# One fused encoder step on Trainium2: attention re-cut into steps of one chunk and one key group, with four query tiles placed between them

## The chip, the core and the metric

The kernel runs on one core of one Trainium2 chip. The metric is the device time of one execution in microseconds (us). The engines are named as in the profile: PE (matrix products), PEld (its weight loads), DVE (vector), ACT (scalar), POOL (GpSimd) and SP (issues most DMAs). All operands are float32. In projections each operand is split into a rounded part (`hi`, type fp32r) and a rest (`lo`), and three products `hi*hi + hi*lo + lo*hi` are summed; inside attention plain float32 products are used.

## What is computed

The reference is a two-layer trunk for two request groups: one prompt of 512 rows and 8 streams of 16 new rows, so 640 rows of width 1024. Layer 0 is gated linear attention and a convolutional FFN; layer 1 is windowed attention over shared keys and values, and again the FFN. The change touches the windowed attention and the end of both mixers' output projections. Cut to that part:

```
def sink_attention(q, k, v, valid, sinks):
    s = einsum('bqngd,bknd->bngqk', q, k)
    m = maximum(max(s, -1), sink)
    e = exp(s - m)
    p = e / (sum(e, -1) + exp(sink - m))
    return einsum('bngqk,bknd->bqngd', p, v)
# prompt: 8 chunks of 64 queries; a chunk sees its own 64 keys and the 128 before it (fewer for chunks 0 and 1)
# streams: 16 queries see 128 cached keys and their own 16
# 16 query heads of 64 in 2 key groups (8 heads share one key and value head)
x = x + attention(rmsnorm(x) @ w_q, ...) @ w_o
x = x + conv_ffn(rmsnorm(x))
```

## The kernel before

The program is written out by hand as one instruction list per engine, with semaphores between them. Each engine works its own list in order, so the order in the source is the schedule. The residual `X` and its two parts `XH`, `XL` lie with features on partitions: 8 tiles of 128 x 640. A projection to 128 output features is a **tile**: `fm_tile` (L359 to L373, products at L368) runs 8 feature blocks x 3 products x 2 halves of 320 columns, 48 matmuls into one of four pairs of PSUM banks; `fm_half` (L375, L379) does one half of it. Weight tiles are brought by SP in pairs (`later_piece`, L864), rounded by ACT (`round_tile`, L344, L348), and their rest is taken by DVE (`rest_tile`, L351, L355); four weight slots rotate.

**Attention stage** (`att_*`, L870 to L1261). PE makes keys and values (`tm_unit`), four query tiles, transposes keys and cached keys (L944, L952), then makes the other four query tiles (L955, products at L368). DVE scales each query tile into `QF` (L1135) and copies the transposed keys into `KTD` (L1125) and `KCT` (L1126, L1131). Then come 40 **steps**: 32 of the prompt (chunk `c`, two neighbouring query tiles, which is four heads of one key group) and 8 of one stream each. For a step:

- PE `scores` (L959): two products, one per half of the array's rows (64 each), into two banks (L972); in a stream step two products of full height with zero-padded queries `QZ` (L979).
- DVE `maxima` (L1142): a row maximum over both banks (L1147), the sink (L1149, L1151) and the sign (L1152).
- ACT `exponentials` (L1216): two exponentials with a running sum (L1223) and one for the sinks (L1224).
- DVE `normalise` (L1154): sum (L1157), reciprocal (L1159), two scalings of the probabilities (L1163).
- PE `transposes` (L984, L992), ACT `to_sbuf` (L1226, L1237 or L1241), PE `values` (L996): per half of the probabilities one product over 128 window keys and one over 64 own keys (L1007); in a stream step one over 128 cached keys (L1016) and one over 16 new ones (L1018). The value operand `VZ` carries 64 zero columns, so that each product fills all 128 output partitions.
- ACT `round_out` (L1244, L1248) and DVE `rest_out` (L1166, L1170) write the result as `XH`, `XL`.

The loops are skewed: in round `n`, PE does `scores(n)`, `transposes(n-2)`, `values(n-3)`; DVE `maxima(n)`, `normalise(n-1)`, `rest_out(n-4)`; ACT `round_out(n-4)`, `to_sbuf(n-2)`, `exponentials(n)`. Scores, transposed probabilities and results each alternate between two places, so `scores(n)` waits for `exponentials(n-2)`. DVE also copies the stream queries into `QZ` (L1176), and POOL has cleared `QZ` and the zero columns (L907).

After the last steps PE makes the output projection: the first half of its tile 0 between the last steps (L1030), the other half (L1036), and tiles 1 to 7 (L1038). DVE adds each tile to `X` (`add_x`, L493). **Resplit**: when all eight tiles are done, ACT rounds the eight blocks of the new `X` (`round_x`, L436) and DVE takes the rests (`rest_x`, L440), because `XH` is still read by the last tile; the FFN's first tile waits for each block's rest. The same two helpers (`add_and_resplit`, L453, and `square_and_resplit`, L463) serve the output projection of layer 0.

```
            act.wait_ge(full, u0 + KT)
            for k in range(KT):
                if k == 2:
                    round_tile(act, n0 + 4 + KT - 1)
                ...
                round_x(act, k, vec)
```

Of the kernel before, what the change touches and what calls it, by code (L numbers as in the profile page):

```python
# [45 lines left out]
def build(nc, A, O):  # L46
    ctx = ExitStack()
    with ctx:
# [63 lines left out]
        NM = sb("neg_max", [128, 2, 2])  # L112
        SE = sb("sink_exp", [128, 2, 2])
        ES = sb("exp_sum", [128, 2, 2])
# [63 lines left out]
        P = at("probs", [128, 2, 512], F32, e_area)  # L178
        PT = at("probs_cols", [128, 2, 512], F32, e_area + 4096)
        KTD = at("keys_cols", [128, KVH, SEQ], F32, e_area + 8192)  # L180
        VZ = at("v_0_v", [128, TT - 1, KVH, 3 * HD], F32, e_area + 12288)
        QZ = at("q_0_q", [128, NS, KVH, 2, 4, SL], F32, e_area + 18432)
# [3 lines left out]
        V4 = at("v_new_rows", [128, KVH, 2, HD], F32, d_area + 5120)  # L186
        VN = at("v_new", [SL, NS, KVH, 2, HD], F32, d_area + 6144)
        VCD = at("cache_v", [128, NS, KVH, 2, HD], F32, DRAW_AREA)
        VS = at("v_0_v_shifted", [128, TT - 1, KVH, 3 * HD], F32, k_area)
# [16 lines left out]
        free = sem("free")  # L206
        hi_done = sem("hi_done")
# [79 lines left out]
        a_pt = sem("a_pt")  # L287
        a_o = sem("a_o")
# [23 lines left out]
        U_AO = U_KC + 6  # L312
# [18 lines left out]
        NATT = (TT - 1) * KT + NS  # L331
# [27 lines left out]
        def fm_tile(pe, n0, u0, i=0, wstep=4, ustep=4, fresh=None, beside=None):  # L359
            pe.wait_ge(lo_done, n0 + 1 + wstep * i)  # L360
            if u0 >= 4:
                pe.wait_ge(free, u0 - 3 + ustep * i)
            for k in range(KT):
                if fresh is not None:
                    pe.wait_ge(xl_done, fresh + k + 1)
                for a, (w, x) in enumerate(((WH, XH), (WH, XL), (WL, XH))):
                    for f in range(2):
                        mm = pe.matmul(PS[:, 2 * (u0 % 4) + f, 0:HALF], w[:, n0 % 4, k, :],  # L368
                                       x[:, k, f * HALF:(f + 1) * HALF],
                                       start=(k == 0 and a == 0), stop=(k == KT - 1 and a == 2))  # L370
            if beside is not None:
                mm = beside()
            mm.then_inc(full, 1)  # L373
# [79 lines left out]
        def add_and_resplit(v, n0, u0, vec, base):  # L453
            for j in range(KT):
                add_x(v, j, u0 + j)
                if j < KT - 1:
                    rest_tile(v, n0 + 4 + j)
            for k in range(KT):
                if k == 2:
                    rest_tile(v, n0 + 4 + KT - 1)  # L460
                rest_x(v, k, vec, base)

        def square_and_resplit(act, n0, u0, norm, vec):  # L463
# [5 lines left out]
            act.wait_ge(full, u0 + KT)  # L469
            for k in range(KT):  # L470
                if k == 2:
                    round_tile(act, n0 + 4 + KT - 1)
                if k == 4:
                    act.wait_ge(free, u0 + KT)
                    square_x(act, KT - 1, norm)
                if k == KT - 1:
                    act.wait_ge(free, u0 + KT)
                round_x(act, k, vec)

# [390 lines left out]
        def att_sp(sp):  # L870
# [12 lines left out]
            sp.dma_start(VS[0:CH, :], VZ[CH:128, :]).then_inc(s_vs, 16)  # L883
            sp.dma_start(VS[CH:128, 0:TT - 2], VZ[0:CH, 1:TT - 1]).then_inc(s_vs, 16)
            for dup in range(2):
                for g in range(KVH):
                    sp.dma_start(VCD[:, :, g, dup, :], A["cache_v"][:, :, g, :].rearrange("s k d -> k s d")).then_inc(s_vn, 16)
# [6 lines left out]
            for s in range(NS):  # L894
                r = slice(SL * s, SL * s + SL)
                sp.dma_start(O["k_s"][s, WIN - SL:WIN], KD[r, TT - 1, :, 0, :]).then_inc(s_out, 16)
                sp.dma_start(O["v_s"][s, WIN - SL:WIN], V4[r, :, 0, :]).then_inc(s_out, 16)
            sp.dma_start(O["k_p"][0], KD[:, TT - 2, :, 0, :]).then_inc(s_out, 16)
            sp.dma_start(O["v_p"][0], VZ[:, TT - 2, :, 0:HD]).then_inc(s_out, 16)
# [7 lines left out]
        def att_pool(pool):  # L907

            pool.wait_ge(free, U_KV)
            pool.wait_ge(s_tout, 128)  # L910
            pool.memset(QZ[:, :, :, :, :, :], 0.0).then_inc(azero, 1)
            pool.memset(VZ[:, :, :, HD:2 * HD], 0.0).then_inc(azero, 1)

# [5 lines left out]
        def att_pe(pe):  # L919
# [17 lines left out]
            for j in range(1, 4):  # L937
                fm_tile(pe, T_AQ + j, u_q(j))
# [16 lines left out]
            for j in range(4, 8):  # L955
                fm_tile(pe, T_AQ + j, u_q(j))
            pe.wait_ge(s_vs, 16 * 2)

            def scores(n):  # L959
                if n >= 2:  # L960
                    pe.wait_ge(a_ex, n - 1)
                if n < 2:

                    pe.wait_ge(free, u_q(5 + n) + 1)
                if n == 3:
                    pe.wait_ge(free, u_q(7) + 1)
                if n < NATT - NS:
                    c, m, g = step_of(n)
                    k0, nk = window(c)
                    for a in range(2):  # L970
                        h = slice(HD * a, HD * a + HD)
                        mm = pe.matmul(PS[:, score_bank(n) + a, 0:nk], QF[h, m // 2, c, :, :].rearrange("p m q -> p (m q)"),  # L972
                                       KTD[h, g, k0:k0 + nk], start=True, stop=True, tile_position=(HD * a, 0))
                else:
                    s = n - (NATT - NS)
                    if s == 0:
                        pe.wait_ge(qz, 16)
                    for g in range(KVH):
                        mm = pe.matmul(PS[:, score_bank(n) + g, 0:WIN + SL],  # L979
                                       QZ[:, s, g, :, :, :].rearrange("p e m t -> p (e m t)"), KCT[:, g, s, :],  # L980
                                       start=True, stop=True)
                mm.then_inc(a_sc, 1)

            def transposes(n):  # L984
# [3 lines left out]
                if n >= 2:  # L988
                    pe.wait_ge(a_pt, n - 1)
                for a in range(2):  # L990
                    for x, k in enumerate(key_parts(n)):
                        mm = pe.transpose(PS[0:k, prob_bank(n), 256 * a + 128 * x:256 * a + 128 * x + 128],  # L992
                                          P[:, n % 2, 256 * a + 128 * x:256 * a + 128 * x + k], ident[:, :])
                mm.then_inc(a_tr, 1)

            def values(n):  # L996
                pe.wait_ge(a_pt, n + 1)
                if n >= 2:
                    pe.wait_ge(a_ol, n - 1)
                b = out_bank(n)  # L1000
                if n < NATT - NS:
                    c, m, g = step_of(n)
                    ops = [(a, x, k) for a in range(2) for x, k in enumerate(key_parts(n))]
                    for j, (a, x, k) in enumerate(ops):
                        vv = VS if c % 2 and c > 1 else VZ
                        t = max(c // 2 - 1, 0) + x
                        mm = pe.matmul(PS[:, b, 0:128], vv[0:k, t, g, HD * a:HD * a + 128],  # L1007
                                       PT[0:k, n % 2, 256 * a + 128 * x:256 * a + 128 * x + 128],
                                       start=(j == 0), stop=(j == len(ops) - 1))
                else:  # L1010
                    s = n - (NATT - NS)
                    if s == 0:
                        pe.wait_ge(s_vn, 16 * (NS + 4))
                    for g in range(KVH):
                        o = PS[:, b, 128 * g:128 * g + 128]
                        pe.matmul(o, VCD[:, s, g, :, :].rearrange("p e d -> p (e d)"),  # L1016
                                  PT[:, n % 2, 256 * g:256 * g + 128], start=True, stop=False)
                        mm = pe.matmul(o, VN[:, s, g, :, :].rearrange("p e d -> p (e d)"),  # L1018
                                       PT[0:SL, n % 2, 256 * g + 128:256 * g + 256], start=False, stop=True)
                mm.then_inc(a_o, 1)  # L1020

            for n in range(NATT + 3):
                if n < NATT:
                    scores(n)
                if n == NATT + 1:
# [3 lines left out]
                    pe.wait_ge(a_ol, 4 * HALF // CH)  # L1029
# [3 lines left out]
                if n >= 3:  # L1033
                    values(n - 3)
            pe.wait_ge(a_ol, NATT)
            fm_half(pe, T_AO, U_AO, 1).then_inc(full, 1)  # L1036
            for j in range(1, KT):
                fm_tile(pe, T_AO + j, U_AO + j)  # L1038

        def score_bank(n):
            return 2 * ((U_AO + n % 2) % 4)

        def prob_bank(n):
            return 2 * ((U_AO + 2) % 4) + n % 2
# [3 lines left out]

        def u_q(j):  # L1050
            return U_Q + j + (4 if j >= 4 else 0)

        def step_of(n):
            c, m = n // 4, 2 * (n % 4)
            return c, m, m // 4
# [4 lines left out]
        def key_parts(n):  # L1063

            if n >= NATT - NS:
                return [WIN, SL]
            nk = window(step_of(n)[0])[1]
            return [nk] if nk <= 128 else [128, nk - 128]

        def heads_out(n, a):  # L1070

            b = out_bank(n)
            if n < NATT - NS:
                c, m, _ = step_of(n)
                return [PS[:, b, 0:128].rearrange("p (m q) -> p m q", m=2)] + \
# [1096 lines left out]
```

## Time and profile before

| | us |
|---|---|
| median of 3 runs (lowest, highest) | 1546.15 (1545.23, 1547.86) |
| the profiled execution: its time | 1542.32 |
| its span, first to last instruction | 1540.6 |
| last four query tiles begin | 862.76 |
| 40 attention steps | 891.1 to about 997 |
| output tiles 1 to 7 begin | 1002.87 |
| FFN of layer 1, first tile begins | 1054.08 |

### The profile page before, as it was taken

How to read it: one execution, taken by the hardware profiler on the slowest of the kernel's cores; microseconds unless marked ns; L12 is line 12 of the kernel's file. 1: busy time of each engine (PE TensorE's matmuls, PEld its weight loads, DVE VectorE, ACT ScalarE, POOL GpSimd, SP SyncE). 2: the span in 40 equal slices, each digit the busy share in tenths (PEclk: the TensorE clock that was granted, in tenths of full speed). 3: DMA queues.
4: the chain of work that ended last, by engine and by line, in shares of the span. 5: the costliest groups of instructions: out<-in, count | busy, mean ns of one | idle time of the engine just before them, and what ended most of it. 6: DMA issues, size and time to landing. Idle time of an engine off the chain costs nothing.

```text
span 1540.6 us, 26157 instructions
## 1 busy us (share of the span) xinstructions
PE 1487.6 (97%) x10213; PEld 1442.7 (94%) x10213; DVE 975.0 (63%) x1748; ACT 563.4 (37%) x989; POOL 169.4 (11%) x186
## 2 busy tenths in 40 slices
PE   7999998999999999999998989999999999999996
PEld 6988998999999999999998967899999999999996
DVE  4366676448666666676577378536766666666655
ACT  4145354434232323233343157524333332323222
POOL 1013220121000000000032000021000000000000
PEclk9999999999999999999999989999999999999999
DMA  6421333432222122112206300021222222212102
GB/s 227 128 83 57 112 102 101 136 110 83 82 82 82 54 82 82 58 51 81 83 1 142 116 28 1 13 83 55 84 81 82 82 82 82 82 64 72 54 1 93
DMA packets 104360, 122.17 MB, mean 79 GB/s; under 512 B 13315, under 2 KB 96201, under 8 KB 104025
## 3 DMA queue, kind: packets, MB, share of 16 engines
q1 hardware_dynamic: 104188, 121.27, 24.4%
q8 instruction: 43, 0.70, 0.2%
q14 instruction: 21, 0.16, 0.0%
q10 hardware_dynamic: 108, 0.03, 0.0%
HBM read 109.43 MB, written 11.95 MB: 79 GB/s over the span
## 4 chain that ended last, share of the span: by engine, by line
PE 91%; DVE 5%; ACT 2%; issue 1%; POOL 0%; DMA 0%; SPq 0%; DVEq 0%; ACTq 0%
PE ps L368 54%; PE ps L529 18%; PE ps L1764 7%; PE ps L1007 2%; DVE x_lo L440 1%; PE ps L547 1%; PE ps L992 1%; PE ps L379 1%; PE ps L393 1%; PE ps L1809 1%; PE ps L972 1%; PE ps L1822 1%; PE ps L1846 1%; PE ps L1842 0%; DVE x_res L493 0%
## 5 line engine op out<-in xcount | busy, mean ns | idle before, releaser
L368 PE MATMUL ps<-x_hi,w_hi 128*128 128x320 f32 x1888 | 431.3, 310 | 7.4 <-DVE x_lo L440 6.9
L368 PE MATMUL ps<-x_lo,w_hi 128*128 128x320 f32 x1888 | 430.2, 309 | 0.0
L368 PE MATMUL ps<-x_hi,w_lo 128*128 128x320 f32 x1888 | 430.2, 309 | 0.0
L368 PEld LDWEIGHTS ps<-x_hi,w_hi 128*128 128x128 f32 x1888 | 315.4, 188 | 9.4 <-issue 4.7
L368 PEld LDWEIGHTS ps<-x_hi,w_lo 128*128 128x128 f32 x1888 | 315.7, 188 | 0.0
L368 PEld LDWEIGHTS ps<-x_lo,w_hi 128*128 128x128 f32 x1888 | 315.6, 188 | 0.0
L348 ACT ACTIVATE w_hi<-w_raw 128x1024 fp32r<-128x1024 f32 x138 | 145.0, 1060 | 423.4 <-PE ps L368 382.2
L493 DVE TENSOR_TENSOR x_res<-x_res,ps 128x640 f32<-128x640 f32 x192 | 153.7, 817 | 130.1 <-PE ps L368 66.1
L355 DVE TENSOR_TENSOR w_lo<-w_raw,w_hi 128x1024 fp32r<-128x1024 f32 x138 | 169.7, 1236 | 33.6 <-ACT w_hi L348 26.4
L611 DVE TENSOR_TENSOR up_rows<-ps,rstd_cols 128x320 f32<-128x320 f32 x88 | 43.1, 490 | 164.6 <-PE ps L368 164.6
L529 PE MATMUL ps<-gated_hi,d_hi 128*128 128x320 f32 x640 | 145.8, 309 | 0.0
L529 PE MATMUL ps<-gated_lo,d_hi 128*128 128x320 f32 x640 | 145.7, 309 | 0.0
L529 PE MATMUL ps<-gated_hi,d_lo 128*128 128x320 f32 x640 | 145.6, 309 | 0.0
L807 POOL TENSOR_TENSOR tail_cols<-up_rows,ones 128x4 f32 (+1 forms) x44 | 51.2, 1164 | 827.7 <-DVE up_rows L613 773.5
L529 PEld LDWEIGHTS ps<-gated_hi,d_hi 128*128 128x128 f32 x640 | 107.0, 188 | 0.0
L529 PEld LDWEIGHTS ps<-gated_lo,d_hi 128*128 128x128 f32 x640 | 106.9, 188 | 0.0
L529 PEld LDWEIGHTS ps<-gated_hi,d_lo 128*128 128x128 f32 x640 | 106.9, 188 | 0.0
L745 ACT ACTIVATE d_hi<-d_raw 128x512 fp32r<-128x512 f32 x88 | 54.7, 628 | 138.7 <-PE ps L529 138.7
L1764 PE MATMUL ps<-w_hi,x_hi 128*128 128x256 f32 x320 | 93.5, 292 | 4.8 <-DVE log_gate L1595 2.6
L733 ACT ACTIVATE conv_out<-up_rows,conv_taps 128x656 f32<-128x656 f32 x88 | 82.2, 935 | 37.6 <-DVE up_rows L613 35.8
L1764 PE MATMUL ps<-w_lo,x_hi 128*128 128x256 f32 x320 | 91.7, 286 | 0.0
L1764 PE MATMUL ps<-w_hi,x_lo 128*128 128x256 f32 x320 | 91.6, 286 | 0.0
(269 smaller groups left out, 1901.3 us busy)
## 6 DMA issues: line engine op xcount, KB each, us to landing
w_raw<-in_ffn_w_up_dram SPq DMA_DIRECT2D x44, 1024.0 KB, 5.2
d_raw<-in_ffn_w_down_dram SPq DMA_DIRECT2D x22, 1024.0 KB, 5.0
w_raw<-in_gla_w_in_dram SPq DMA_DIRECT2D x12, 1024.0 KB, 6.1
seq_states<-in_state_gla_dram SPq DMA_DIRECT2D x4, 1024.0 KB, 5.5
out_dram<-seq_states SPq DMA_DIRECT2D x4, 1024.0 KB, 8.3
w_raw<-in_gla_w_out_dram SPq DMA_DIRECT2D x4, 1024.0 KB, 5.3
w_raw<-in_att_w_q_dram SPq DMA_DIRECT2D x4, 1024.0 KB, 6.8
w_raw<-in_att_w_o_dram SPq DMA_DIRECT2D x4, 1024.0 KB, 5.0
```

What stands on the lines that cost most here:

```text
L348: act.activation(WH[:, n0 % 4, :, :], WRAW[:, p0 % 2, :, half:half + 128], ACT.Copy).then_inc(hi_done, inc)
L355: v.tensor_tensor(WL[:, n0 % 4, :, :], WRAW[:, p0 % 2, :, half:half + 128], f32(WH[:, n0 % 4, :, :]), ALU.subtract).then_inc(lo_done, inc)
L368: mm = pe.matmul(PS[:, 2 * (u0 % 4) + f, 0:HALF], w[:, n0 % 4, k, :], x[:, k, f * HALF:(f + 1) * HALF], start=(k == 0 and a == 0), stop=(k ...
L379: mm = pe.matmul(PS[:, 2 * (u0 % 4) + f, 0:HALF], w[:, n0 % 4, k, :], x[:, k, f * HALF:(f + 1) * HALF], start=(k == 0 and a == 0), stop=(k ...
L493: v.tensor_tensor(halves(X[:, m, :]), halves(X[:, m, :]), unit(u0), ALU.add).then_inc(free, inc)
L529: mm = pe.matmul(PS[:, 2 * (w % 4) + f, 0:HALF], wt[:, k, 128 * m:128 * m + 128], y[:, k, f * HALF:(f + 1) * HALF], start=(k == 0 and a == ...
L611: v.tensor_tensor(UB[:, j, 2:2 + HALF], PS[:, b, 0:HALF], RB[:, 0:HALF], ALU.mult)
L733: act.activation(CB[:, j, :], UB[:, j, 0:CC], ACT.Identity, scale=CWT[:, 0, bass.ds(c, 1)], bias=CWT[:, 3, bass.ds(c, 1)]).then_inc(t0_don ...
L745: act.activation(DH[:, :, 256 * c:256 * c + 256], DRAW[:, :, 256 * c:256 * c + 256], ACT.Copy).then_inc(dhi, 1)
L807: pool.tensor_tensor(to[:, :, 0:2], UB[:, a, SEQ:SEQ + 2], ones[:, 0:4].rearrange("p (a r) -> p a r", a=2), ALU.mult)
L1007: mm = pe.matmul(PS[:, b, 0:128], vv[0:k, t, g, HD * a:HD * a + 128], PT[0:k, n % 2, 256 * a + 128 * x:256 * a + 128 * x + 128], start=(j ...
L1764: mm = pe.matmul(PS[:, VR_B[m % 2], 0:DV], x[:, k, 128 * t:128 * t + 128], w[:, n0 % 4:n0 % 4 + 2, k, :], start=(k == 0 and a == 0), stop= ...
```

## The change

- A prompt step is one chunk and one whole key group: eight heads, four products of scores, 16 steps ordered group by group (`ATT_STEPS`). A stream step takes two streams: 4 steps. 20 steps in place of 40; four row sums and maxima per step in place of two.
- Query tiles 4 to 7 (the second group's) are no longer made before the steps. Each of the first eight steps is followed on PE by one half tile (`query_half`), evicted by `query_out`; these use the second pair of score banks, so up to step 8 there is one pair for scores, and `scores(n)` waits for `exponentials(n-1)`.
- `scores(0)` waits until all transposed keys, the cached ones too, are copied (`U_KC + 2`).
- Values: without zero columns. Products have 64 output columns of the array each and 256 moving columns: two over 128 window keys, two over 64 own keys (each in its own quarter of the array). `VP`, `VS` hold values once; a third copy fills the shifted rows.
- Stream queries lie packed in `QS`, written by POOL (a product with ones); scores and values of streams use 64-column pieces. `QZ` and its clearing are gone. Cached values come in one DMA in place of four.
- Transposed probabilities have one place for the window part (copied by ACT) and one for the own part (copied by DVE, `own_to_sbuf`).
- One broadcast product normalises all four heads' blocks.
- Results of the first eight steps go to `QF` (where the first group's queries were) and are split later, tile by tile, in rounds 12 to 15 (`rest_first` and ACT's rounding), since `XH` is still read by the query halves.
- The four output weight tiles formerly prepared under the query tiles are prepared in rounds 2, 4, 6 and 8.
- Output tile 1's first half is made before the second half of tile 0.
- Resplit, in both layers: the last output tile releases each block of `XH` as it is read (`x_free`), and seven of eight blocks are split under that tile.

```diff
-        NATT = (TT - 1) * KT + NS
+        ATT_STEPS = [(c, g) for g in range(KVH) for c in range(SEQ // CH)]
+        NCH, NPR = SEQ // CH, len(ATT_STEPS)
+        NATT = NPR + NS // 2
...
         def fm_tile(...):
-            if beside is not None:
-                mm = beside()
+                if release and k < KT - 1:
+                    mm.then_inc(x_free, 1)
...
         def add_and_resplit(v, n0, u0, vec, base):
-            for j in range(KT):
+            for j in range(KT - 1):
                 add_x(v, j, u0 + j)
-                if j < KT - 1:
-                    rest_tile(v, n0 + 4 + j)
-            for k in range(KT):
-                if k == 2:
-                    rest_tile(v, n0 + 4 + KT - 1)
+                rest_tile(v, n0 + 4 + j)
+            for k in range(KT - 1):
                 rest_x(v, k, vec, base)
+            add_x(v, KT - 1, u0 + KT - 1)
+            rest_x(v, KT - 1, vec, base)
+            rest_tile(v, n0 + 4 + KT - 1)
...
         def square_and_resplit(act, n0, u0, norm, vec):
-            act.wait_ge(full, u0 + KT)
...
+            for k in range(KT - 1):
+                act.wait_ge(x_free, (KT - 1) * (n0 // T_AO) + k + 1)
                 round_x(act, k, vec)
+            act.wait_ge(free, u0 + KT)
+            round_x(act, KT - 1, vec)
+            square_x(act, KT - 1, norm)
+            round_tile(act, n0 + 4 + KT - 1)
...
         def att_pool(pool):
+            for j in range(KT):
+                pool.wait_ge(free, U_Q + j + 1) if j < 4 else pool.wait_ge(q_free, 2 * (j - 4) + 2)
+                for c in range(2):
+                    mm = pool.tensor_tensor(QS[...], QF[...], ones[...], ALU.mult)
+                mm.then_inc(qz, 1)
...
             def scores(n):
+                if n == 0:
+                    pe.wait_ge(free, U_KC + 2)
+                elif n <= NCH:
+                    pe.wait_ge(a_ex, n)
+                else:
+                    pe.wait_ge(a_ex, n - 1)
+                if n == NCH:
+                    pe.wait_ge(q_free, 8)
...
             def values(n):
...
+                    for j in range(4):
+                        s_, g = 2 * (n - NPR) + j // 2, j % 2
+                        for e in range(2):
+                            pe.matmul(PS[HD * e:HD * e + HD, o, ...], VC[:, s_, g, :], PTA[:, b, c], tile_position=(0, HD * e))
+                        for e in range(2):
+                            mm = pe.matmul(PS[HD * e:HD * e + HD, o, ...], VN[:, s_, g, :], PTB[0:SL, b, c], tile_position=(0, HD * e))
...
+                        for a in range(2):
+                            mm = pe.matmul(PS[HD * a:HD * a + HD, o, 0:256], vv[:, t, g, :], PTA[...], tile_position=(0, HD * a))
+                    if w1:
+                        for a in range(2):
+                            mm = pe.matmul(PS[h, o, 0:256], vv[h, t, g, :], PTB[h, b, 0:256], tile_position=(HD * a, HD * a))
...
             for n in range(NATT + 3):
                 if n < NATT:
                     scores(n)
+                if n < NCH:
+                    query_half(n)
...
+            pe.wait_ge(a_ex, NATT)
+            fm_half(pe, T_AO + 1, U_AO + 1, 0)
             pe.wait_ge(a_ol, NATT)
...
             for n in range(NATT + 4):
+                if 1 <= n <= NCH:
+                    query_out(n - 1)
                 if n < NATT:
                     maxima(n)
+                if 2 <= n < NATT + 2:
+                    own_to_sbuf(n - 2)
                 if 1 <= n <= NATT:
                     normalise(n - 1)
+                if n in ROUND_AO:
+                    rest_tile(v, T_AO + ROUND_AO.index(n))
                 if n >= 4:
                     rest_out(n - 4)
+                if 0 <= n - NCH - 4 < 4:
+                    rest_first(n - NCH - 4)
```

## Rows read from the trace of the kernel before

**Rows 1.** Windows: from:to, length, PE, PEld, DVE, ACT, POOL busy, PE clock, DMA.
```profile
891.10:895.20 4.10, 1.68 (x19) 1.21 (x18) 3.44 (x18) 1.64 (x11) 0.00 (x0) 1.00 0.00 0
895.20:908.80 13.60, 12.19 (x58) 8.90 (x57) 11.31 (x57) 8.76 (x43) 0.00 (x0) 0.50 0.23 78
908.80:963.00 54.20, 52.42 (x355) 39.37 (x354) 46.20 (x218) 39.79 (x161) 0.00 (x0) 1.00 0.01 1
...
987.30:990.70 3.40, 3.40 (x14) 3.25 (x13) 0.58 (x2) 0.54 (x2) 0.00 (x0) 0.50 0.00 0
...
997.55:1001.00 3.45, 3.45 (x13) 3.45 (x14) 0.00 (x0) 0.00 (x0) 0.00 (x0) 0.51 0.48 118
```
**Rows 2.** The chain in order of time (start, us, what): two full prompt steps.
```profile
946.35 1.36 PE ps L1007 x7
...
948.74 1.36 PE ps L1007 x7
```
**Rows 3.** The chain again: one stream step, the next one's start, statistics of the FFN.
```profile
980.78 0.44 PE ps L992 x4
981.22 0.22 PE ps L1016 x2
981.44 0.41 PE ps L1018 x2
...
983.37 0.44 PE ps L992 x4
...
1063.49 1.08 PE ps L403 x4
```
**Rows 4.** Timeline of DVE and ACT inside one full prompt step.
```profile
936.27 0.56 DVE L1147 TENSOR_REDUCE neg_max<-ps 128x2 f32<-128x384 f32 x1 [0.31 <-PE ps L972]
...
936.84 0.60 ACT L1237 ACTIVATE probs_cols<-ps 128x512 f32<-128x512 f32 x1 [0.64 <-PE ps L992]
...
937.20 0.15 DVE L1157 TENSOR_TENSOR exp_sum<-exp_sum,sink_exp 128x2 f32<-128x2 f32 x1
937.33 0.42 ACT L1223 ACTIVATE probs<-ps,neg_max 128x192 f32<-128x192 f32 x1
...
937.59 0.55 DVE L1163 TENSOR_SCALAR probs<-probs,exp_sum 128x192 f32<-128x192 f32 x2
...
937.74 0.41 ACT L1223 ACTIVATE probs<-ps,neg_max 128x192 f32<-128x192 f32 x1
...
938.05 0.28 DVE L1170 TENSOR_TENSOR x_lo<-ps,x_hi 128x128 fp32r<-128x128 f32 x1
...
938.13 0.20 ACT L1224 ACTIVATE sink_exp<-sink_exp 128x2 f32<-128x2 f32 x1
```
**Rows 5.** The chain at the entry (four query tiles) and at the exit (seven output tiles).
```profile
862.76 28.41 PE ps L368 x192
...
1002.87 49.29 PE ps L368 x336
```
**Rows 6.** Timeline at the entry: DVE's copies of the transposed keys.
```profile
862.53 0.68 DVE L1125 COPY keys_cols<-ps 128x512 f32<-128x512 f32 x1
...
863.32 2.34 DVE L1131 COPY seq_keys_cols<-ps 128x1024 f32<-128x1024 f32 x2
```
**Rows 7.** The page's costliest groups: DVE's rests of weight tiles.
```profile
L355 DVE TENSOR_TENSOR w_lo<-w_raw,w_hi 128x1024 fp32r<-128x1024 f32 x138 | 169.7, 1236 | 33.6 <-ACT w_hi L348 26.4
```
**Rows 8.** Groups by line and shape from 1052 to 1063.3: xcount | busy, mean ns | idle before.
```profile
L440 DVE SCALAR_TENSOR_TENSOR x_lo<-x_res,vectors,x_hi 128x640 fp32r<-128x640 f32 x8 | 7.9, 1035 | 0.0
L436 ACT ACTIVATE x_hi<-x_res,vectors 128x640 fp32r<-128x640 f32 x8 | 6.1, 816 | 5.4 <-PE ps L368 5.4
...
L368 PE MATMUL ps<-x_hi,w_hi 128*128 128x320 f32 x16 | 3.9, 326 | 2.5 <-DVE x_lo L440 2.5
...
L488 POOL TENSOR_TENSOR sum_sq<-sum_sq,squares 128x640 f32<-128x640 f32 x1 | 2.1, 2062 | 8.0 <-ACT squares L449 8.0
```
**Rows 9.** Waits of PE from 333 to 345, layer 0: total us, times, longest.
```profile
PE ps L368 <- DVE x_lo L440: 2.5, 3, 0.9
```

More of the change, by code:

```diff
@@ L997, in values @@
                 pe.wait_ge(a_pt, n + 1)
+                if both(n):
+                    pe.wait_ge(a_ptb, both(n))
                 if n >= 2:
                     pe.wait_ge(a_ol, n - 1)
[L1000 to L1009, printed above, removed]
-                else:
[L1011 to L1019, printed above, removed]
@@ L1063, in key_parts, with both, keys_of, probs @@
         def key_parts(n):
[L1065 to L1075, printed above, removed]
[L1076 to L1084 removed]
+            if n >= NPR:
+                return True, True
+            c = ATT_STEPS[n][0]
+            return c > 0, c != 1
+        def both(n):
+            return sum(all(key_parts(m)) for m in range(n + 1))
+        def keys_of(n):
+            return window(ATT_STEPS[n][0])[1] if n < NPR else WIN + SL
+        def probs(n, first, count):
+            return P[:, n % 2, first:first + count]
+        def v_rows(chunk, half):
+            if chunk % 2 == half:
+                return VP, chunk // 2
+            return VS, (chunk - 1 - half) // 2 % (TT - 1)
+        def heads_out(n):
+            i_ = PS[:, out_bank(n), 0:256]
+            if n < NPR:
+                c, g = ATT_STEPS[n]
+                return [i_.rearrange("p (m q) -> p m q", m=4)] + \
+                    [x[:, 4 * g:4 * g + 4, CH * c:CH * c + CH] for x in (XH, XL)]
+            c = SEQ + 2 * SL * (n - NPR)
+            return [i_.rearrange("p (s k t) -> p s k t", s=2, t=SL)] + \
+                [x[:, :, c:c + 2 * SL].rearrange("p k (s t) -> p s k t", t=SL) for x in (XH, XL)]
         def att_dve(v):
@@ new lines, in att_dve @@
+            v.reciprocal(RB[:, :], RB[:, :]).then_inc(rstd, 1)
+            v.wait_ge(rstd, RC[2] + 2)
+            for j in range(4):
+                v.wait_ge(full, U_Q + j + 1)
+                v.scalar_tensor_tensor(out=QF[:, j // 2, :, j % 2, :].rearrange("p (a c) q -> p a c q", a=2),
+                                       in0=unit(U_Q + j).rearrange("p a (c q) -> p a c q", q=CH),
+                                       scalar=HD ** -0.5, in1=RB[:, :].rearrange("p (a c q) -> p a c q", a=2, q=CH),
+                                       op0=ALU.mult, op1=ALU.mult).then_inc(free, 1)
+                rest_tile(v, T_AQ + 4 + j)
@@ L1210, in att_act @@
                 round_tile(act, n)
-            for j in range(KT - 1):
-                act.wait_ge(full, u_q(j) + 1)
+            for j in range(4):
+                act.wait_ge(full, U_Q + j + 1)
                 round_tile(act, T_AQ + 4 + j)
@@ L1538, in front_pe @@
             for j in range(4, 8):
[L1539 removed]
+                fm_tile(pe, T_WO + j, U_WO + j, release=j == KT - 1)
         def front_dve(v):
```

348 lines of the change are left out of this document (195 added, 153 removed).

## The prediction

> **What bounds the kernel now.** I read the windows first, to see at which clock PE works, then the chain of waits in the attention stage, then the timeline of one step, then the groups around the resplit. The stage opens badly: from 891.1 to 895.2 PE works 1.7 of 4.1 us, and after that the granted clock is 0.5 (1.2 GHz) for 13.6 us; it is 0.5 again for 3.4 us twice at the end, both times on the halves of output tile 0 [rows 1]. Between, at full clock, the chain stays on PE: one full prompt step takes 948.74 - 946.35 = 2.39 us [rows 2], one stream step 983.37 - 980.78 = 2.59 [rows 3]. So PE sets the pace of the 40 steps, DVE follows with about 2.06 us of work per step (936.27 to 938.33), ACT with 1.6 of copies and exponentials [rows 4].
>
> **Prices on PE.** Four passes of 320 columns take 1.08 us [rows 3], and a float32 product is two passes, so a product of N columns costs N x 1.69 ns: 64 cost 0.11, 128 0.22, 144 0.24, 192 0.32, 256 0.43. Four transposes take 0.44. The first value product after the transposes takes 0.22, the following ones, which alternate between 128 and 16 rows of the array, 0.41 [rows 3]: each change of the array's shape costs 0.2. Check: a prompt step is 4 x 0.11 transposes, 4 x 0.22 values, 0.32 for two half-height score products side by side, 4 changes: 2.44 against 2.39. A stream step gives 0.44 + 0.88 + 0.48 + 0.8 = 2.60 against 2.59.
>
> **The new steps on PE.** Full prompt step: scores 0.64, six transposes 0.66, window values 0.43 and own values 0.43 if the two 64-column products of a pair run side by side, four changes 0.8: 2.96, where two old steps took 4.78. No row shows a 64-column pair. Its ends: side by side 0.43, as the half-height scores do, or one after the other 0.86; I take 0.43 because the score pair is the nearest row. New stream step (two streams): scores 0.96, eight transposes 0.88, eight value pairs of 64 columns at 0.22 (a pass not under the 0.11 of a transpose), ten changes 2.0: 5.6, against 5.18 for two old ones. So the prompt gains and the streams lose.
>
> **The new steps on DVE and ACT.** From 384 to 768 elements at 1.09 ns each (0.56 for 384 against 0.28 for 128 [rows 4]) the maximum takes 0.98; the small operations to the sum 0.37, from there to the scaling 0.39 [rows 4]; one scaling of 768 elements three quarters of the 1.24 that another DVE operation takes for 1024 [rows 7], 0.93; the copy of the own part 0.41 (0.68 for 512 columns [rows 6]); the result 0.42. Sum 3.5; with a 512-column rest of the first group (0.70) 4.2. Four exponentials at 0.41 and the sinks' 0.20 are 1.83 on ACT, the window copy 0.60 [rows 4].
>
> **Part by part**, from 862.76, where the four later query tiles begin, to 1002.87, where seven output tiles remain [rows 5]: 140.1 us before.
>
> 1. *Entry.* `scores(0)` now waits for the last copy of cached keys, 863.32 + 2.34 [rows 6], so PE starts at 865.8: 3.0 later, and nothing lies under it, since `query_half(0)` is queued behind.
> 2. *First group, steps 0 to 7.* A half tile is 24 x 0.148 = 3.55 (28.41 over 192 [rows 5]). With one pair of score banks `scores(n+1)` waits for `exponentials(n)`; ACT's list puts `to_sbuf(n-2)` ahead of it, and that waits for `transposes(n-2)`, which PE does after the half tile. So after the transposes come 0.60 + 1.83 and 0.3 of handing over, 2.7; values (0.86 + 0.4) lie under this, and PE is idle for about 1.2. A full step: scores 0.64, two changes 0.4, half tile 3.55, transposes 0.66, 2.7: 7.95. Steps 0 to 3 have fewer keys or nothing to transpose: 4.2, 4.4, 7.4, 7.6. Sum 23.6 + 4 x 7.95 = 55.4. DVE's evictions of query halves (320 columns, 0.28 + 192 x 1.09 ns = 0.49) and three weight rests (1.24 each [rows 7]) lie under the 7.95.
> 3. *Second group, steps 8 to 15.* Two score banks again; DVE sets the pace, PE's 2.96 lies under it. Step 8 (64 keys, but the last weight rest and query eviction) 4.7, then 2.7, 2.8, 3.1, then four with the first group's rests at 4.2: 30.1.
> 4. *Streams.* 4 x 5.6, the last prompt steps' transposes and values 5.5, waits for DVE in the first two 2.8: 30.7.
> 5. *Output tile 0* 7.1; the wait of 1.3 before its second half is gone, as tile 1's first half covers it.
>
> Sum 865.8 + 55.4 + 30.1 + 30.7 + 7.1 = 989.1 against 1002.87: 13.8 less at full clock.
>
> 6. *Clock.* The old total holds its own slow stretches; the new sum holds none. PE idles 3 us at the entry, as it idled before 895.2, so I charge the first half tile and its neighbours 2.5. Around steps 2 and 3 PE waits 2.6 of 3.8 us: 1.6. The old tail has two stretches at 0.5, each costing half its 3.4 us; the new one has three places like it (the lone half tile, the values after it, tile 1's half): 5.0. Together 9.1; ends 0 and the rival below. Net of the stage: -4.7.
> 7. *Resplit.* PE waited 2.5 us for the rests in layer 1 [rows 8] and 2.5 in layer 0 [rows 9]. Seven blocks now go under the last tile (48 x 0.148 = 7.1 us): ACT starts about 1.9 into it, after one weight rounding and one square, and 0.82 per block [rows 8] ends with PE's last release; DVE's 1.03 per block, overlapping, ends about 1.3 after the tile, while PE does its conv-state transposes and needs block 6 only 5 us into the next tile. Block 7 is ready 3.7 after the tile, needed at 7. Both waits go: -5.0. Ends: -5.0 and 0 if DVE falls behind.
> 8. *Costing nothing.* Fewer value copies on DVE (PE is in a projection); one DMA of cached values in place of three more issues on SP, and one more shifted copy, all before the steps; the later output weights' DMAs, issued from rounds 4 and 8 on, 60 us before use. POOL's 16 small products: at most 2.1 us each (a 640-column sum of this kernel [rows 8]); the last is due 25 us before the streams. If that cover went, `scores(16)` would wait.
>
> Total -4.7 - 5.0, about **-9.5 us**: the profiled 1542.3 becomes about 1533, and since it lies 3.8 under the median, 1537 on the scale of the runs shown. A measurement of this kernel can tell about 0.2% (3.1 us) from no change.
>
> **Rivals.**
>
> *A. The stage keeps its clock.* Neither the entry's wait nor the short steps bring 0.5, and only the tail's two old stretches remain (3.4): -13.8 + 3.4 - 5.0 = -15.4, 1531. For: a half tile every 8 us. Against: the entry looks like 891 to 895.
>
> *B. The 64-column pairs run one after the other.* Stream steps gain 0.96 + 1.76 = 2.7 each, 10.9 in all, less the 2.8 of waits; steps 8 to 11 another 2; the first group hides it (1.7 + 0.4 under 2.7). +10: no change, 1546.5. For: two products of one pair share a bank, which the old score pairs never do. The Trainium skill, "TensorEngine Tiling (Array Packing)", section on restrictions and gotchas, says that different row tiles cannot access the same bank at the same time; by that rule the own-value pairs and the stream scores (different row halves, one bank) would serialize, 3.8 us of this rival, while the window pairs would not. No row here has such a pair, so the trace neither supports nor contradicts it.
>
> *C. Slower: the clock stays at 0.5 from step 8 through the streams.* There is no half tile any more; PE's products use half or a quarter of the array and wait for DVE. Its 8 x 2.96 + 4 x 5.6 = 46 us of work would double, less some 9 us of waiting: +37 throughout, +18 if half of it. With half, -9.5 + 18 is about +9: 1555. It decides from some 19 us more at 0.5 than charged. For: the old steps with few keys stayed at 0.5 for 13.6 us with PE nearly always occupied [rows 1]. Against: the full old steps kept 1.0 for 54 us.
>
> **Chances.** Forecast 0.48, A 0.17, B 0.18, C 0.17. Of the forecast's 0.48 (1530 to 1544) nearly all is faster by over 0.2%, all of A, a quarter of B: 0.66. Within 0.2%: half of B and the upper edge of the forecast with a little of C, 0.17. Slower: the rest of B and most of C, 0.17. The range runs from 1528 (A with a slightly better tail) to 1551 (B's upper part and the lower part of C); C's worse half and a stage better than A are left out, under 0.2.
>
> **What would show it.** Right: `scores` in the first group preceded by waits on the sinks' exponential of 1 to 2.5 us; steps 12 to 15 at about 4.2 with DVE without idle time; stream steps near 5.6 at full clock; no waits of L368 on `x_lo` after an output projection. Wrong: value pairs at 0.86 (B), a clock of 0.5 over most of 920 to 985 (C), or the FFN's first tile still stuttering.

## The result, and the profile after

The changed kernel takes 1525.2 us (median of 4 runs, 1518.9 to 1526.7) beside 1545.75 before: ratio 0.9857, interval 0.9828 to 0.9886, 20.5 us faster. The forecast was 1537, range 1528 to 1551. The direction was right; the gain is more than twice the one forecast, and the time lies 2.8 us below the range.

The profiled execution takes 1525.38, its span 1523.4 (before: 1542.32 and 1540.6). So 17.2 us lie between the two profiles, and I account for these first. Windows of the changed kernel where PE's clock fell, and one stretch before such a fall (from:to, length, PE, PEld, DVE, ACT, POOL busy, PE clock, DMA share, GB/s):

```profile
810.00:816.80 6.80, 6.10 (x29) 6.10 (x29) 2.37 (x5) 1.84 (x3) 1.62 (x1) 0.51 0.28 58
...
830.35:833.76 3.41, 3.41 (x16) 3.41 (x15) 3.41 (x5) 3.41 (x6) 0.00 (x0) 0.53 0.00 0
...
864.45:871.30 6.85, 5.43 (x24) 5.32 (x25) 2.19 (x6) 1.38 (x9) 0.00 (x0) 0.52 0.35 110
...
885.00:888.40 3.40, 3.40 (x14) 3.40 (x15) 3.26 (x9) 0.00 (x0) 0.00 (x0) 0.52 0.00 0
...
902.00:905.50 3.50, 3.50 (x16) 3.50 (x15) 2.90 (x7) 0.00 (x0) 0.00 (x0) 0.53 0.37 123
...
926.00:929.40 3.40, 3.40 (x18) 1.80 (x16) 2.44 (x8) 1.69 (x10) 0.08 (x1) 0.52 0.02 5
...
973.10:980.60 7.50, 7.50 (x82) 6.48 (x78) 1.39 (x4) 1.36 (x3) 0.00 (x0) 1.00 0.00 1
980.60:987.40 6.80, 6.80 (x40) 6.22 (x39) 0.57 (x2) 0.38 (x1) 0.00 (x0) 0.51 0.27 69
```

In place of [rows 1] with its 13.6 us at 0.5 in one piece there are now short stretches behind places where PE waited, and one at 980.6 behind a stretch in which PE was busy all the time: with a half output tile on the whole array up to 976.9, then with transposes and products of 64 columns on 128 or 16 rows of the array. Not every wait is followed by a fall: the clock stayed at 1.0 behind the wait of 1.2 us before 917.64.

The chain of the changed kernel, in order of time (start, us, what):

```profile
829.68 29.94 PE ps L378 x192
...
863.55 2.27 DVE seq_keys_cols L1257 x2
865.87 1.12 PE ps L983 x8
866.98 5.77 PE ps L389 x24
...
909.96 0.92 PE ps L983 x8
910.88 3.71 PE ps L389 x24
...
915.03 0.23 PE ps L1019 x2
...
944.65 0.88 DVE neg_max L1189
...
947.83 0.53 ACT x_hi L1340
948.39 0.69 DVE x_lo L1229
949.08 0.88 DVE neg_max L1189
...
982.59 13.02 PE ps L389 x72
995.61 42.24 PE ps L378 x288
1037.85 0.82 PE ps L577 x11
...
1038.90 7.23 PE ps L378 x48
1046.14 1.08 PE ps L413 x4
```

It answers to [rows 2, 3, 5]. Read it from the top. At the entry PE waits for the last copy of cached keys until 865.87. A full step of the first group is 917.64 - 909.96 = 7.68: scores, half tile, transposes, and then 2.4 us until the copy and the exponentials on ACT are done. PE makes the values of an earlier step under these and is idle for the last 1.2 us, as the timeline says (in brackets the idle time and what ended it):

```profile
917.64 0.92 PE L983 MATMUL ps<-keys_cols,q_cols 64*128 64x192 f32 x8 [1.23 <-ACT sink_exp L1307]
```

In the second group (steps 12 to 15) the chain goes round over DVE's maxima, ACT's exponentials, ACT's rounding of the first group's results, DVE's rest. At the end PE goes from the last output tile over the conv-state transposes (L577) straight into the FFN; nothing like the 2.5 us of [rows 8] is left.

PE in the middle of a stream step's values, by the timeline of the changed kernel; the last two figures of a product are the rows and columns of the array that it uses:

```profile
971.00 0.34 PE L1039 MATMUL ps<-probs_cols_window,cache_v 128*64 128x64 f32 x4
971.27 0.33 PE L1043 MATMUL ps<-probs_cols_own,v_new 16*64 16x64 f32 x4
971.53 0.34 PE L1039 MATMUL ps<-probs_cols_window,cache_v 128*64 128x64 f32 x4
```

A pair of 64-column products (two passes each, the two products side by side) takes 0.265 from start to start, switch of rows included. The forecast had 0.42.

| part | forecast | profile after |
|---|---|---|
| PE starts the steps | 865.8 | 865.87 |
| first group, with its share of the clock (4.1) | 59.5 | 59.7 |
| second group | 30.1 | 28.2 |
| streams, output tile 0, tail clock (5.0) | 42.8 | 34.8 |
| seven output tiles left at | 998.2 | 988.6 |
| resplit, layer 0 and layer 1 | -2.5, -2.5 | -2.8, -3.0 |
| clock at layer 1's keys, values, first queries | 0 | +2.9 |

(988.6 is 995.61, where six tiles are left, less 42.24/6; the second group runs from 925.52 to 953.73 by the weight loads of its scores.) The stage gives 1002.87 - 988.6 = 14.3, the resplit 5.8, less 2.9: the 17.2 of the spans.

### The profile page after: what moved, and what is told of

Its sections match the earlier page's. It is cut to its first block, busy times and chain, and to the rows that moved or that the text cites. A ratio compares the mean times of both kernels' runs of the same rounds, so it can differ in the third digit from the quotient of the medians.

```text
span 1523.4 us, 25733 instructions
## 1 busy us (share of the span) xinstructions
PE 1460.1 (96%) x10169; PEld 1417.4 (93%) x10169; DVE 958.0 (63%) x1543; ACT 544.4 (36%) x909; POOL 174.5 (11%) x200
## 4 chain that ended last, share of the span: by engine, by line
PE 90%; DVE 5%; ACT 2%; issue 1%; POOL 0%; DMA 0%; ACTq 0%; DVEq 0%
PE ps L378 52%; PE ps L536 18%; PE ps L1845 7%; PE ps L389 4%; PE ps L554 1%; ACT probs L1305 1%; PE ps L403 1%; DVE x_lo L450 1%; PE ps L1890 1%; PE ps L1903 1%; PE ps L983 1%; PE ps L1927 1%; PE ps L1923 0%; DVE x_res L500 0%; DVE neg_max L1189 0%
## 5 line engine op out<-in xcount | busy, mean ns | idle before, releaser
L378 PE MATMUL ps<-x_hi,w_hi 128*128 128x320 f32 x1808 | 413.3, 310 | 1.9 <-DVE x_lo L450 1.9
L378 PE MATMUL ps<-x_hi,w_lo 128*128 128x320 f32 x1808 | 412.5, 309 | 0.0
L378 PE MATMUL ps<-x_lo,w_hi 128*128 128x320 f32 x1808 | 412.5, 309 | 0.0
L378 PEld LDWEIGHTS ps<-x_hi,w_hi 128*128 128x128 f32 x1808 | 302.8, 188 | 2.6 <-issue 2.1
L378 PEld LDWEIGHTS ps<-x_hi,w_lo 128*128 128x128 f32 x1808 | 302.8, 188 | 0.0
L378 PEld LDWEIGHTS ps<-x_lo,w_hi 128*128 128x128 f32 x1808 | 302.8, 188 | 0.0
```

## The experiments

Each kernel ran beside the kernel before on the same chip, on three chips in all (medians of the kernel before there 1544.4 to 1544.7). The control ran on one of them, so some of the differences from it below are taken across chips. Runs of one kernel spread over 4 to 8 us; of the kernels made from the changed one only the last two lie clear of all the control's runs, and for the others the stage in the profile has to say where the time went. "Stage" is from the first transpose of the keys to the FFN's statistics in each profile: before 204.0, changed kernel 186.5.

| kernel | median, us | runs | stage |
|---|---|---|---|
| changed, again | 1522.4 | 1519.3 to 1526.9 | 186.5 |
| before + resplit | 1537.8 | 1534.7 to 1541.7 | 197.9 |
| changed, old resplit in layer 0 | 1526.3 | 1524.0 to 1530.1 | 186.5 |
| query halves ahead of the steps | 1522.9 | 1519.3 to 1523.7 | 187.0 |
| tile 1's half undone | 1527.5 | 1522.7 to 1528.1 | 187.1 |
| stream values grouped | 1518.1 | 1515.5 to 1519.7 | 179.2 |
| first scores' wait shortened | 1517.2 | 1514.6 to 1521.2 | 179.9 |
| first rests a round later | 1518.4 | 1517.9 to 1521.9 | 181.3 |
| transposes first | 1507.5 | 1504.9 to 1511.4 | 170.5 |
| the last four together | 1497.6 | 1496.2 to 1500.9 | 160.2 |

**The control.** The changed kernel itself.

> The changed kernel itself, as a control on the same chip as the three kernels beside it. Four runs of it took 1518.9 to 1526.7 us with mean granted clocks of 0.986 to 0.979: 0.001 of clock is 3.05 us at half speed, so up to 1.5 us of time. Theory: its runs spread over 1519 to 1527 again and line up with their clocks by about 1.5 us per 0.001; in its profile other stretches are at 0.5 than in the first one (810 to 817 and 831 to 834 are not bound to come back, those behind an idle PE between 865 and 930 are). Rival: the stretches belong to the code; then the same ones come back in the same places.

Its windows where the first profile had lost 2.9 us, and its first and last stretch at 0.5 in the steps:

```profile
815.30:818.70 3.40, 3.40 (x16) 3.40 (x17) 1.64 (x4) 1.12 (x2) 1.32 (x1) 0.50 0.11 23
829.00:862.00 33.00, 31.07 (x217) 30.89 (x216) 21.46 (x29) 11.51 (x14) 5.26 (x7) 1.00 0.40 123
866.50:873.30 6.80, 5.62 (x25) 5.50 (x26) 1.95 (x5) 1.38 (x9) 0.00 (x0) 0.50 0.32 99
...
982.60:989.40 6.80, 6.80 (x39) 6.30 (x36) 0.42 (x1) 0.38 (x1) 0.00 (x0) 0.50 0.26 69
```

At the keys and values the theory holds: one short stretch as in the kernel before, the first query tiles at full clock. So the 2.9 us are not bound to the code; but they are not of one execution alone either, for the profile of "tile 1's half undone" below has both stretches again (0.50 from 812.4 to 819.2 and from 832.9 to 836.3), and no other one has them. The five from the entry to the tail came back, each at the same distance from the first scores (865.87 there, 867.7 here; the first begins 1.2 ahead of them, the last 115 behind, in both). For the last one, behind a busy PE, that is the rival's outcome. The runs line up with the mean granted clock: 1526.9 at 0.981 and 1519.3 at 0.986, 1.5 us per 0.001 (1.0 to 1.6 by the runs of the kernel before on two of the chips).

**Before, with the resplit alone.** `fm_tile` releases blocks, `add_and_resplit` and `square_and_resplit` as in the change.

> The kernel before with one part of the change alone: the last output tile of each layer releases the blocks of the split residual as it reads them, and seven of eight blocks are split under it. The changed kernel's profile shows PE's statistics 2.8 us earlier behind the layer 0 projection and another 3.0 us gained behind the layer 1 projection, but between the two layers 2.9 us are lost again at a granted clock of 0.5 (keys, values and first query tiles of layer 1). Theory: the layer 0 gain is swallowed there, so this kernel is about 3.0 faster than before in its profile. Rival: the loss there belongs to the attention part; then this kernel gains the full 5.8.

Measured 0.9957 (0.994 to 0.9973) of before, 6.9 us: the rival, the full 5.8 and a little more. The swallowing that I had read into one profile falls. From the end of the last output tile of layer 0 to the FFN's statistics this kernel takes 8.3 us, where the kernel before takes 11.3 (333.18 to 344.50):

```profile
334.59 0.82 PE ps L570 x11
...
342.88 1.08 PE ps L406 x4
```

Behind layer 1's it takes 8.3 as well (before: 11.3). In this execution the two stretches at 0.5 on the halves of output tile 0 [rows 1] were missing as well, though nothing had been changed there:

```profile
980.00:1005.00 25.00, 23.73 (x150) 21.21 (x150) 8.41 (x29) 8.03 (x29) 1.91 (x1) 1.00 0.08 20
```

**Changed, with the old resplit in layer 0.**

```diff
-            add_and_resplit(v, T_WO, U_WO, V_FFN, XF[0])
+            old_add_and_resplit(v, T_WO, U_WO, V_FFN, XF[0])
-            square_and_resplit(act, T_WO, U_WO, 1, V_FFN)
+            old_square_and_resplit(act, T_WO, U_WO, 1, V_FFN)
```

> The changed kernel with the old resplit in layer 0 only (layer 1 keeps the new one). Theory: the waits of 2.5 us on the rests come back behind the layer 0 projection, but layer 1's keys, values and first query tiles then run as in the kernel before (first four query tiles 28.4 us, not 29.9), so the time is within 1 us of the changed kernel's 1525. Rival: the slow clock there has another cause, and the kernel is 2.8 us slower than the changed one, 1528.

Medians: 3.9 slower than the control, 1.1 slower than the changed kernel's first four runs. The first query tiles took 28.4, as the theory said, but so they did in the control with the new resplit; the rival's 2.8 fits. Behind layer 0's output tiles the 11.3 us are back:

```profile
333.06 0.84 ACT x_hi L446
...
344.36 1.08 PE ps L413 x4
```

Together with the run above: the resplit is worth about 3 us per layer, and none of it is swallowed.

**Query halves ahead of the steps.**

```diff
+            for n in range(NCH):
+                query_half(n)
             for n in range(NATT + 3):
                 if n < NATT:
                     scores(n)
-                if n < NCH:
-                    query_half(n)
```

> The changed kernel with the eight half query tiles ahead of all steps in place of between them, and two pairs of score banks from the start; steps, values and tail as in the changed kernel. Theory: in the changed kernel the half tiles hid little, since a full step of 7.68 us is the half tile's 3.7 plus a chain of 4.0 that they do not cover, so 28.4 us of half tiles and eight steps at DVE's pace of 3.3 to 3.9 give about 57 in place of 59.7 us, and the time stays within 3 us of the changed kernel's 1522. Rival: the half tiles are where the gain came from; then up to 28 us less the waits are lost again, over 10 slower.

No difference: 1522.9 beside 1522.4, stage 187.0 beside 186.5. Two things differ here, the place of the half tiles and the second pair of score banks that this place leaves free from the start. In the changed kernel's order, then, the half tiles between the steps cover nothing on balance. PE's longest waits from 885 to 985 in this kernel (total us, times, longest):

```profile
PE ps L1012 <- DVE probs L1202: 12.9, 11, 3.6
PE ps L1047 <- DVE q_cols L1216: 4.4, 3, 2.0
```

They stand in place of the changed kernel's waits between the half tiles, from 872 to 926:

```profile
PE ps L983 <- ACT sink_exp L1307: 8.2, 5, 2.2
PE ps L983 <- DVE q_cols L1234: 1.5, 1, 1.5
```

So the change's gain in the stage does not come from the place of the query tiles. What is left are, above all, the larger steps (20 of them, products without zero columns, fewer small DVE and ACT operations); that is an argument by elimination, for no run takes the larger steps out alone.

**Transposes first.** This mends that order.

```diff
                 if n < NATT:
                     scores(n)
+                if 2 <= n < NCH:
+                    transposes(n - 2)
                 if n < NCH:
                     query_half(n)
...
-                if 2 <= n < NATT + 2:
+                if NCH <= n < NATT + 2:
                     transposes(n - 2)
```

> The changed kernel with the transposes of step n-2 ahead of the half query tile of round n, not behind it, in rounds 2 to 7. In the changed kernel PE waits 1.7 to 2.4 us before the scores of steps 3 to 8 (12.2 us in all), because ACT's copy and the exponentials of a step come after the transposes and these after the half tile. Theory: under the half tile they cost nothing, a full step takes 6.1 us in place of 7.68, and about 12 us go, 3 more if the two stretches at 0.5 that follow such a wait go too: 1510 to 1513. Rival: DVE's maxima, query evictions and weight rests then set a pace close to the old one, and less than 5 us go.

The chain over one full step:

```profile
897.43 0.85 PE ps L983 x8
...
899.09 3.51 PE ps L389 x24
902.61 0.58 PE ps L1051 x4
903.19 0.58 PE ps L1058 x4
903.77 0.85 PE ps L983 x8
```

6.34 in place of 7.68, on PE alone and without a wait: copy and exponentials now run under the half tile. 14.9 us faster than the control, 16.0 in the stage. The first group, from its first scores to those of step 8, takes 46.2 in place of 59.7, 13.5 less. 3.1 of it is the clock, as the theory had it; no stretch at 0.5 is left between 870 and 917:

```profile
869.40:917.20 47.80, 45.88 (x339) 37.67 (x338) 31.80 (x83) 22.16 (x85) 2.39 (x8) 1.00 0.09 28
```

The other 10.4 stand against the theory's 12 (the waits that it put at 12.2 are 9.7 by the profile's own count above, 8.2 and 1.5). The rest of the stage's 16.0 is the tail, which ran at full clock here with its code unchanged.

**Stream values grouped.** All four window pairs, then all four own pairs.

```diff
+                    for part in range(2):
                         for j in range(4):
...
-                                      start=True, stop=False, tile_position=(0, HD * e))
+                                      start=part == 0 and j == 0, stop=part == 1 and j == 3, tile_position=(0, HD * e))
```

> The changed kernel with the products of a stream step's values in another order: first the four window pairs (128 rows of the array), then the four own pairs (16 rows). Theory: in the changed kernel a pair of 64-column products is two passes of 0.055 and the switch between 128 and 16 rows adds 0.155, so 0.265 each and 2.1 per step; with one switch in place of eight a step's values take about 1.0. The last two stream steps are paced by PE, so 2.2 us are gained, up to 4.3 if all four are. Rival: the 0.265 is the price of a pair whatever stands before it; then the values stay at 2.1 and the time does not move.

```profile
972.77 2.49 PE ps L1041 x64
975.25 10.75 PE ps L389 x72
```

Two steps' values take 2.49, 1.24 each in place of 2.10. In the old order a step has eight changes of rows, seven inside and one behind it; here it has two. The timeline of one step, four pairs of each kind, parts the two prices:

```profile
966.89 0.69 PE L1041 MATMUL ps<-probs_cols_window,cache_v 128*64 128x64 f32 x16
967.50 0.68 PE L1041 MATMUL ps<-probs_cols_own,v_new 16*64 16x64 f32 x16
968.11 0.41 PE L389 MATMUL ps<-x_hi,w_hi 128*128 128x320 f32 x1
```

Four pairs and one change take 0.61, where one pair and one change took 0.265: a pair alone 0.115, a change 0.15. So the change of rows is what costs, and six fewer give about the 0.86. The order in which a pair adds to what the pair before it has just written, which the edit alters too, is not the cause: the change costs 0.15 here as well, where the two pairs beside it write different columns. 4.3 us less than the control by the medians, 7.3 in the stage; the steps account for about 2.6 of it. The rest is clock: the three halves behind the steps (10.75, not 13.02) and the half tile at the entry, which the edit does not touch, ran at 1.0 here.

**First scores' wait shortened** (`free` of `U_KT + 2` in place of `U_KC + 2`).

> The changed kernel with the first scores waiting for the copies of the prompt's keys alone, not for those of the cached keys (one wait's number changed). Theory: PE starts the first step 2.3 us earlier (863.5 in place of 865.9), the first maxima follow when DVE has copied the cached keys (865.9), and nothing else moves: 2.3 us faster; and if the clock of 0.5 from 864.5 to 871.3 came from that idle time, another 2 us. Rival: the chain over the maxima and exponentials of step 0 is what sets the pace, and the gain is under 1 us.

5.2 us less than the control, 6.6 in the stage. Scores begin 4.3 after the first key transpose in place of 6.6: the theory's 2.3. No stretch at 0.5 follows there, as its clock part had it; but "stream values grouped" has none there either, with the old wait, so that the clock's 2 us come from the shorter wait is not shown. The other stretches were shorter too (3.4 us at the tail, none at 902).

**First group's rests a round later on DVE** (`rest_first(n - NCH - 5)`).

> The changed kernel with the rests of the first group's results one round later on DVE. In the changed kernel steps 12 to 14 take 3.8 to 4.4 us, where DVE waits 0.5 for ACT's rounding, which stands behind the exponentials of the same step. Theory: this wait goes, the steps become 3.9, and 1.5 to 2 us go in all. Rival: the stream steps behind take the work up again (DVE is as full there), and under 0.7 go.

4.1 us less than the control by the medians. In this kernel the wait of DVE for ACT's rounding, in the changed kernel from 936 to 956

```profile
DVE x_lo L1229 <- ACT x_hi L1340: 1.4, 3, 0.5
```

is gone, and a step takes 3.9. From the scores of step 12 to those of step 19 it takes 25.1 us in place of 27.4, so the edit itself gives 2.3; the rest of the 5.2 in the stage came from the tail, at full clock in this profile with the code unchanged.

**Tile 1's half undone.**

> The changed kernel with output tile 0's second half ahead of tile 1 again. Theory: PE then waits for the last rests, as in the kernel before (1.3 us there), so it is 1 to 2 us slower than the changed kernel, 1523 to 1525, more if the idle time brings another stretch at 0.5. Rival: the values of the last steps end late enough that the rests are there, and the time does not move.

```profile
984.97 0.39 ACT x_hi L1318
...
985.39 0.43 DVE x_lo L1220
...
985.87 5.59 PE ps L389 x24
```

PE waits 0.9 (forecast 1.3), and the stage is 0.5 longer. By the medians it is 5.1 slower, but its runs overlap with the control's, and its profile has the two stretches at the keys and values: something between 0.5 and 5, not settled.

**All four together.**

> The changed kernel with the stream values grouped, the first scores' wait shortened, the transposes ahead of the half tiles and the first group's rests one round later. Theory: the four gains stand on separate stretches and add up: 2.6 (stream values in the profile of that kernel) + 2.3 + 12 + 1.5, 18 us, and the clock falls less often: 1503 to 1508. Rival: once PE waits less, DVE becomes the bound of the first group too, and the sum stays under 12.

1497.6, ratio 0.9704 (0.9687 to 0.972) to before and 24.8 us under the control: better than expected. The windows of the first group and the second:

```profile
861.00:905.00 44.00, 43.69 (x320) 37.46 (x320) 29.60 (x74) 20.10 (x81) 2.33 (x8) 1.00 0.16 51
905.00:931.00 26.00, 20.71 (x166) 12.17 (x166) 23.19 (x66) 19.64 (x79) 0.07 (x1) 1.00 0.13 42
```

PE is busy 43.7 of 44 us in the first group, DVE 23.2 of 26 in the second, and in this execution the stage has no stretch at 0.5, in the streams and the tail no more than in these two windows. The stage is 26.3 us shorter than the changed kernel's. What the four gave each in its own profile without the clock is 2.6, 2.3, 10.4 and 2.3, 17.6 together, and the changed kernel's stretches cost 8 to 9 (next section); the two come to the 26.3, so it is the clock that goes beyond the 18 us expected of the four.

## Why the prediction was right and wrong

The forecast's gain was 9.5 us, the measured one 20.5. Of the 11 between them 8.0 are the streams with the tail, 3.4 the scale, 1.9 the second group and 0.8 the resplit; the clock at layer 1's keys took back 2.9.

**The price of the new stream step was the main fault** (the paragraph on the new steps on PE). It set "eight value pairs of 64 columns at 0.22 (a pass not under the 0.11 of a transpose)" and a change at 0.2: 3.36 per step for the values. Measured 2.10. A pair of 64 columns takes 0.115 without the change ("stream values grouped"), half of the 0.22, since cost goes with the columns as the forecast's own rule said; the floor was added without a row for it. A change between these short passes costs 0.15, not 0.2. Four steps: 5.0 of the 8.0 us that this part was dearer than measured. Another 2.1 is the tail's clock, 2.9 against 5.0 charged (13.02 against 10.75 for three halves, and 0.6 on the last four value groups). What is left is small: scores and transposes took 2.0 a step against 2.24, and the waits for DVE 2.6 against 2.8.

**Right.** The entry to 0.1 us. The first group, by its own chain: transposes, copy, exponentials, handing over (step 7.68 forecast 7.95, PE idle for 1.2 in both). The resplit, 5.8 against 5.0.

**Right by luck.** The sum of the clock: 5.1 in the first group (5.77, 5.25 and 5.25 for half tiles of 3.71) against 4.1, 2.9 in the tail against 5.0, up to 1 at 926 against nothing: 8 to 9 against 9.1, with misses that offset each other. So too the first group's total, 59.7 against 59.5: 1.0 more of clock, about 0.9 less without it (54.5 against 55.4).

**The second group** was right in size (28.2, forecast 30.1), half wrong in cause. DVE was to be without idle time; in steps 12 to 15, at 4.43 from one maximum to the next (949.08 - 944.65; forecast 4.2), it waits 0.5 each for ACT's rounding. ACT's place in the chain had been left out. "First rests a round later" takes that wait away, and the steps come to 3.9.

**The scale.** The forecast carried -9.5 from the profile to the median by adding 3.8, as if the changed kernel's profiled execution would also be 3.8 below its median. It was at its median (1525.38 beside 1525.2). Both profiled executions are single draws; the changed kernel's runs spread over 8 us, in line with the granted clock; 3.4 us of the miss (20.5 against 17.2) are this.

**The rivals.** B falls: the pairs run side by side. Own-value products of two row halves, which write one bank, start together:

```profile
915.76 0.43 PE L1058 MATMUL ps<-probs_cols_own,v_shifted 64*64 64x256 f32 x1
915.77 0.43 PE L1058 MATMUL ps<-probs_cols_own,v_prompt 64*64 64x256 f32 x1
```

The rule of the Trainium skill, "TensorEngine Tiling (Array Packing)", restrictions and gotchas, that different row tiles cannot access one bank at the same time, is not borne out by this trace: the two start 7 ns apart and take no longer than a pair of window products, which share all rows: 0.58 for either pair with its change (L1058 and L1051 in the chain of "transposes first"), where one product after the other is 0.86 by the forecast's own price. The two write different halves of the bank's partitions; whether the rule holds for two that write the same ones is not shown here. C falls: from step 8 through the streams 0.5 held for 3.4 us behind step 8 and then from 980.6 on. A's time was the nearest, but not its reason: the clock did fall, and cost in sum what was charged; PE's work was cheaper.

## What to carry to other kernels

Work put between steps hides a chain only if what starts the chain stands ahead of it: the half tiles bought nothing behind the scores, and behind the transposes they made the first group 13.5 us shorter. Price a product by its columns from the nearest row, and do not add a floor that no row shows; where two prices (pass and switch) are drawn from one row, look for a second row that parts them. Before scaling a forecast from a profile, ask where that one execution lies in the spread of its kernel, and read a clock stretch as the code's only when a second execution has it too.

## What the runs showed of the hardware

The place where the granted clock falls is not fixed by the code alone. In [rows 1] output tile 0 was at 0.5 twice; with the same code there it was at 1.0 all through in another kernel's run. The stretch at 980.6 came while PE was busy 7.5 of 7.5 us, with a half tile on the whole array and then with transposes and passes of 64 columns: being busy did not keep the clock. In the control it came again at the same distance from the first scores; in "transposes first" and "first rests a round later", with the same products in the same order there, it did not come. So one profile without a stretch does not show that an edit removed it. With 64-column products the change between 128 and 16 rows costs more than the passes: 0.15 beside 0.115 for a pair, and six changes fewer took 0.86 off a step of 2.10.
